# A two-block transformer kernel: bias tables read back later, from a row kept in other memory, the mask added just ahead of the softmax, and output weights split ahead of two softmaxes

## The reference

```python
def second_block(x, rel_bias, ...):
    for layer in range(2):
        y = mixer_ab(h, ..., rel_bias) if layer % 2 == 0 else mixer_c(h, ..., rel_bias)
        h = layer_norm(ALPHA * h + y, ...)
        h = layer_norm(ALPHA * h + hier_moe(h, ...), ...)

def mixer_ab(x, w_in, gate_b, conv_w, head_g, w_out, rel_bias):
    p = einsum('bsd,de->bse', x, w_in)                 # queries, keys, values, gates
    ya = dilated_attention(aq, ak, av, rel_bias)       # 8 heads, logits + bias[distance], mask, softmax
    yb = sigmoid(bo) * head_norm(mlstm(bq, bk, bv, bi, bf), head_g)   # 4 heads, after a causal conv
    return einsum('bse,ed->bsd', concatenate([ya, yb]), w_out)

def mixer_c(x, w_in, gate_b, cmp_pos, cmp_w1, cmp_w2, w_out, rel_bias):
    # 8 heads, each with three attentions: over compressed keys, selected blocks and a window
    return einsum('bse,ed->bsd', g0 * o_cmp + g1 * o_slc + g2 * o_win, w_out)
```

## Time and profile before

| | before |
|---|---|
| time, median of 3 runs | 2688.43 us (2686.18 to 2688.82) |
| time of the profiled execution | 2687.73 us |
| its span, first to last instruction | 2685.9 us |
| TensorE busy | 2512.0 us, 94% |
| VectorE busy | 1714.9 us, 64% |
| ScalarE busy | 1081.9 us, 40% |
| mean granted TensorE clock | 0.961 |
| phase ab, from its first matmul to its last norm | about 1470 to 1672 us |
| phase c | about 2077 to 2278 us |

### The profile page before, as it was taken

The page is one execution under the profiler, slowest core; times in us unless marked ns, Lnnn a source line. Parts: engine busy times, 40 slices in busy tenths (PEclk is TensorE's granted clock), DMA queues, the critical chain, the costliest instruction groups (busy, mean ns, idle before and its releaser), DMA issues.

```text
span 2685.9 us, 38028 instructions
## 1 busy us (share of the span) xinstructions
PE 2512.0 (94%) x16084; PEld 2221.0 (83%) x16084; DVE 1714.9 (64%) x2324; ACT 1081.9 (40%) x1294; POOL 81.5 (3%) x116
## 2 busy tenths in 40 slices
PE   4999989999999998999999599999999988999998
PEld 3999758999998778997999487788887957788886
DVE  5887276876877255544656275547886455647985
ACT  2333145334332032223334253436774243446773
POOL 0000000000000003430000000000000000000000
PEclk9999989999999999999999698899999989999999
DMA  6886303874785330001653520646994510647991
GB/s 286 325 322 221 118 24 124 300 277 156 305 298 206 126 110 1 1 2 67 248 177 140 146 96 1 251 188 267 370 368 185 182 68 1 251 188 285 372 369 54
DMA packets 48272, 501.91 MB, mean 187 GB/s; under 512 B 4968, under 2 KB 9448, under 8 KB 10856
## 3 DMA queue, kind: packets, MB, share of 16 engines
q1 hardware_dynamic: 42480, 490.52, 48.1%
q10 hardware_dynamic: 5624, 8.97, 1.3%
HBM read 496.33 MB, written 3.15 MB: 186 GB/s over the span
## 4 chain that ended last, share of the span: by engine, by line
PE 80%; DVE 10%; DMA 4%; ACT 2%; issue 2%; POOL 1%; ACTq 0%; DVEq 0%; POOLq 0%
PE PS L1178 24%; PE PS L565 24%; PE PS L635 6%; PE PS L611 4%; PE PS L528 2%; DMA bias_scratch<-work 2%; PE PS L915 2%; PE PS L928 2%; PE PS L924 1%; DMA ring<-stream 1%; PE PS L648 1%; PE PS L1272 1%; PE PS L548 1%; DVE work L1814 1%; DMA xT<-x_in 1%
## 5 line engine op out<-in xcount | busy, mean ns | idle before, releaser
L565 PE MATMUL PS<-x_part_hi,w_up_hi 128*128 128x256 f32 x1408 | 404.5, 287 | 11.8 <-DVE x_part_lo L1885 6.5
L565 PE MATMUL PS<-x_part_lo,w_up_hi 128*128 128x256 f32 x1408 | 399.4, 284 | 0.0
L565 PE MATMUL PS<-x_part_hi,w_up_lo 128*128 128x256 f32 x1408 | 399.4, 284 | 0.0
L2409 DVE TENSOR_TENSOR ring_low<-ring,m_w_up 128x2048 fp32r<-128x2048 f32 x128 | 293.1, 2291 | 134.0 <-ACT m_w_up L1664 134.0
L1664 ACT ACTIVATE m_w_up<-ring 128x2048 fp32r<-128x2048 f32 x128 | 245.3, 1916 | 187.4 <-PE PS L1178 187.3
L565 PEld LDWEIGHTS PS<-x_part_hi,w_up_hi 128*128 128x128 f32 x1408 | 271.1, 193 | 15.1 <-issue 8.0
L565 PEld LDWEIGHTS PS<-x_part_lo,w_up_hi 128*128 128x128 f32 x1408 | 271.3, 193 | 0.0
L565 PEld LDWEIGHTS PS<-x_part_hi,w_up_lo 128*128 128x128 f32 x1408 | 271.1, 193 | 0.0
L1178 PE MATMUL PS<-m_w_up,xg_hi 128*128 128x512 f32 x640 | 253.0, 395 | 3.8 <-DVE work L2423 3.8
L1178 PE MATMUL PS<-ring_low,xg_hi 128*128 128x512 f32 x640 | 254.0, 397 | 0.0
L1178 PE MATMUL PS<-m_w_up,xg_lo 128*128 128x512 f32 x640 | 253.2, 396 | 0.0
(11 more groups left out here) (519 smaller groups left out, 5245.8 us busy)
## 6 DMA issues: line engine op xcount, KB each, us to landing
ring<-stream SPq DMA_DIRECT2D x133, 2048.0 KB, 7.8
ring<-stream SPq DMA_DIRECT2D x88, 1536.0 KB, 6.6
work<-stream SPq DMA_DIRECT2D x48, 1024.0 KB, 7.6
hT<-stream SPq DMA_DIRECT2D x16, 1024.0 KB, 7.3
ring<-stream SPq DMA_DIRECT2D x3, 1152.0 KB, 5.6
const<-const_tables ACTq DMA_DIRECT2D x1, 2336.5 KB, 18.5
bias_scratch<-work ACTq DMA_DIRECT2D x1, 2048.0 KB
work<-bias_scratch ACTq DMA_DIRECT2D x2, 1024.0 KB, 6.8
```

The costliest lines, as they stand in the source:

```text
L565: last = mm(out, w[a][:, lo:lo + P], x[b][:, at:at + T], start=start and i == 0, stop=stop and i == 2, skip_group_check=skip)
L2409: tt_(ring_low[n][:, part], ring[n][:, part], m_w_up[g % 3][:, :].bitcast(F32), ALU.subtract).then_inc(S("up_split"), 1)
```

## The change

It has four parts. First, the 8 bias rows are kept at `A_Y` and no longer in the middle of `dd`, and VectorE no longer waits for the write to HBM (`bias_stored`) before it fills `dd`. Second, ScalarE's wait for `bias_stored` and the read-back move from behind the gates' logarithm (ahead of half 5) to behind the copy of the sixth piece `ab_in.1` (ahead of half 14). Third, VectorE's wait for the read-back (`bias_in`) and the addition of the mask move from the middle of the mlstm to just ahead of `attention`. Fourth, halves of the output weights move: in `ab` the low part of half 15 from behind step 0 of the attention to ahead of it, and that of half 16 from step 4 to step 5; in `c` both parts of halves 10 and 11 from steps 6 to 10 to ahead of the attention (on ScalarE between the two copies L1763), and of half 12 from steps 12 and 13 to steps 6 and 7.

```diff
-                row = W(A_LS + 512, 512, 0, 8)
+                row = W(A_Y, 512, 0, 8)
...
                 fn(t, t, ACT.Ln, bias=ones[:, 0:1]).then_inc(S("softlog_ready"), 1)
-                act.wait_ge(S("bias_stored"), 16)
-                load_bias(A_BM)
                 mix_highs("ab", 5)
...
                 mix_highs("ab", 13)
                 copied(1, W(A_K, 1024), 0)
+                act.wait_ge(S("bias_stored"), 16)
+                load_bias(A_BM)
                 mix_highs("ab", 14)
...
                     fn(W(C_RAW + kv * T, T, 0, 2 * NCMP), bank(4 + 2 * kv, T, T, 0, 2 * NCMP),
                        ACT.Copy).then_inc(S("cmp_raw"), 1)
+                    if kv == 0:
+                        mix_highs("c", 10, 11)
...
-                attention("c", {i: [lambda i=i: mix_highs("c", i // 3 + 8)] for i in (6, 9, 12)})
+                attention("c", {6: [lambda: mix_highs("c", 12)]})
...
-                dve.wait_ge(S("bias_stored"), 16)
                 dd = ls(256, 1024)
...
                 done(tt_(wk, wk, m1, ALU.subtract), "stab_ready")
-                dve.wait_ge(S("bias_in"), 32)
-                bm = W(A_BM, 8 * ATT).rearrange("p (h c) -> p h c", c=ATT)
-                done(tt_(bm, bm, C("dilated").unsqueeze(1).broadcast_to([P, 8, ATT]), ALU.add))
                 line.next("lexp_ready")
...
-                mix_lows("ab", 14)
-                attention("ab", {0: [lambda: mix_lows("ab", 15)], 4: [linear_out, lambda: mix_lows("ab", 16)], 6: [linear_low]})
+                mix_lows("ab", 14, 15)
+                dve.wait_ge(S("bias_in"), 32)
+                bm = W(A_BM, 8 * ATT).rearrange("p (h c) -> p h c", c=ATT)
+                done(tt_(bm, bm, C("dilated").unsqueeze(1).broadcast_to([P, 8, ATT]), ALU.add))
+                attention("ab", {4: [linear_out], 5: [lambda: mix_lows("ab", 16)], 6: [linear_low]})
...
                 dve.wait_ge(S("c_copied"), 6)
-                attention("c", {i: [lambda i=i: mix_lows("c", (i - 1) // 3 + 8)] for i in (7, 10, 13)})
+                mix_lows("c", 10, 11)
+                attention("c", {7: [lambda: mix_lows("c", 12)]})
```

## The result

The changed kernel takes 2654.14 us (median of 4 runs, 2652.52 to 2656.22) beside 2688.41 for the kernel before (4 runs, 2686.18 to 2688.82): a ratio of 0.9875, 95% interval 0.9858 to 0.9892, so 34.3 us less. Its profiled execution took 2655.35 us, its span is 2653.6 and the mean granted clock 0.970 (before: 2687.73, 2685.9 and 0.961). The forecast was 2660, in a range of 2654 to 2667, whose lower edge the result only just clears.

A forecast was written before the change was run, and what follows sets the result against it. TensorE, busy 94%, was held 33.45 us at L1039 by the bias rows' write to HBM. Terms -28.1 + 4.4 - 4.8 = -28.5 gave 2659.2 us for the profiled execution, near 2660 for the median, range 2654 to 2667.

The forecast's parts named there:

- Part 1: At L1039, moving ScalarE's wait for the write lets half 5 start earlier: 28.1 us saved, 5.3 us of wait left.
- Part 2: Row at `A_Y`, no VectorE wait before `dd`: makes the earlier half 5 pay off, by itself costs and gives nothing more.
- Part 3: Read-backs behind `ab_in.1`: no wait, but issuing takes ScalarE 1.13 us and moves L1637 as much; +0.3 us comes through.
- Part 4: Mask and half 15 ahead of phase ab's attention delay the first maximum: +4.4 us including the read-backs' 0.3, bounds 3.4 to 6.8.
- those counted for half 16: Phase ab's attention: half 16 one step later moves one transpose earlier and one later, 0.2 us (0 to 0.8).
- 4.2 us remain: Phase ab's attention: of the first maximum's 6.0 us delay, TensorE's 1.80 us wait ahead of the fourth scores goes.
- the lower bound: Phase ab's attention: 3.4 us, if only VectorE's sum counts, 3.36 us more work.
- nothing is made up there: Phase ab's attention, fifth and later items: TensorE at half clock, busy 20.18 of 20.70 us, recovers none of the delay.
- Part 5: Phase c: halves 10 and 11 ahead of the attention cost nothing and shorten its transposes' spacings: -4.8 us, bounds -2.1 to -6.2.
- The clock: At L1039 TensorE's clock still falls in the remaining 5.3 us wait, and 2.4 us for half clock behind are still paid.
- The case in which the dear attention carries half clock into the output weights: Rival, 20%: phase ab's output weights lose 2.4 us at half clock and phase c may give only 2.1: 2665 us.

The follow-up runs named there:

- row_only: Kernel before with the bias row at `A_Y` and without VectorE's wait for the write, ScalarE's wait untouched: 2689.67 us, ratio 0.9990 to 1.0021.
- only_c: Kernel before with the edits of phase c alone: 2683.12 us, ratio 0.9974 to 0.9997.
- dve_wait: Changed kernel with VectorE's wait for the write put back ahead of `dd`: 2668.42 us, ratio 0.9908 to 0.9948.
- fit: Changed kernel with the mask in VectorE's mlstm gap, read-backs a half earlier, 24 idle matmuls in each of TensorE's two waits: 2651.52 us.
- again: The changed kernel, unaltered, measured once more in more rounds: 2656.16 us, ratio 0.9866 to 0.9903.
- no_c: Changed kernel with phase c as in the kernel before: 2661.93 us, ratio 0.9886 to 0.9917.

## Why the prediction was right, and where it was off

**Part 1, the stall: 28.1 forecast, 28.0 measured.** The chain named for the remaining wait (TensorE's half 3, ScalarE's half 5, VectorE's gates) is the one that the new chain shows, start by start: half 5 at 1494.59 for 1495.5, L1039 at 1505.57 for 1506.5, the difference being the 1.0 that the execution had gained ahead. In every variant in which ScalarE's wait stands behind half 5, L1039 is early; where it stayed ahead of half 5 (`row_only`, `only_c`), it is not. `ab_in.6` was just in time, at 2.03 us of ScalarE's idle time.

**Part 2, VectorE's wait: the claim was too broad.** The prediction said that it "would hold VectorE at 1508 until 1522", which is what `dve_wait` shows (1506.5 to 1522.46), but also that taking it away "is what makes part 1 work". It is not: with the wait L1039 is as early as without. It guards what comes behind, 9 to 12 us of the 28, and it is worth nothing while ScalarE waits (`row_only`).

**Part 3: the read-backs, +0.3 forecast, nothing measured.** They are issued at 1560.62 (1562 forecast) with no wait. The mis-sized step is that issuing takes ScalarE 1.13 us and moves L1637 by as much. That was read where ScalarE had nothing else to do; here its queue issues them while the copy L1589 runs (1560.61 to 1561.63), and L1637 comes 28.6 us earlier where TensorE comes 28.9, so it is moved by 0.3. VectorE's reduction behind L1640 starts at 1572.84 for 1601.71, the full 28.9 us earlier: its shorter wait (1.71 for 1.98) has taken up the rest.

**Part 4: the attention, +4.4 forecast for parts 3 and 4 together, +3.4 measured.** The third scores came 5.6 us later against the first ones (6.0), but the fourth only 3.4 (4.2). Of the 1.0 us too much, 0.3 are part 3's, 0.1 lies in the rounded lengths, 0.2 are those counted for half 16, which cost nothing, and 0.4 are the step "4.2 us remain": the first two maxima are 1.24 us apart where they were 3.44, so half 15's move gives back its whole 2.2 us behind the first maximum and not only TensorE's wait of 1.80. It cancels in full, and the mask's 3.36 us are the price, which was the lower bound. The prediction's "nothing is made up there" held: what the fourth scores lost, the output weights lost.

**Part 5: phase c, -4.8 forecast, -5.2 measured**, by the spacings 8.20, 6.82, 6.87 for 8.22, 6.87, 6.87. The 0.35 us on top are between items 18 and 21 (7.22 before, 6.87 now), which the sum had left out. The 3.6 of `only_c` lies inside the bounds as well, and so does the 5.3 between the middle traces with and without these edits.

**The clock.** That it still falls in the wait of 5.4 us was right, and so was the price: from L1039 to L1045 the changed kernel takes 14.17 us and `fit`, with the wait filled, 11.80, so 2.4 us. The case in which the dear attention carries half clock into the output weights did not come about.

**The sum.** -28.5 forecast, -29.7 at the edited places, -32.3 in the profiled spans and -34.3 in the medians. The sum of the terms was right within 1.2 us. What lies beyond it was not caused by an edit that I could find: it is in unchanged stretches, whose time differs between executions of one kernel (`again` ends 12.9 us behind the changed kernel's trace, with the same mlstm and the same attention to within 0.02 us). `no_c` and `only_c` together give 29.3, near the sum, and `again` 31.0. So 2654 was reached partly by luck of the executions, and why the unchanged stretches were kind in both medians of the first comparison stays open.

## What to carry to other kernels

When a long wait goes, ask what is late next and add up its starts from rows of the same trace: the remaining 5.3 us came out to 0.1. An operation moved from hidden time to the place just ahead of the first maximum costs its whole length, while two pieces that only change places there cancel. Here a wait of 5.4 us on TensorE cost its length and some 2 us more for the clock, and filling it with the right number of idle matmuls got those back; those too many cost their whole excess.

## What the hardware showed that I had not expected

The granted clock stays low in an attention in which TensorE is busy for 25.32 of 25.70 us, with weight loads busy for 15.24 of them, and is full over the output weights behind it, where the loads are busy for all of 23.20. What decides between the two no run here separates. Filling the wait ahead of it delays the fall (1.00 for the first 10 us in `fit`) but does not prevent it (0.65 over the next 19.7). And a wait of 16 us on VectorE reached TensorE as two waits of 6.4 us together and cost 9.35 us in the trace and 12.3 in the medians. Issuing a DMA on ScalarE's queue, 1.07 us for two, went on beside a running copy of 1.02 us and held the next instruction up by 0.3.
